# Output projection and the following norm as one stage, token tile by token tile

## What is computed

```
def rms_norm(x, g):
    return x * rsqrt(mean(x * x, axis=-1) + 1e-6) * g

for layer in (0, 1):
    x = x + gate_m * (mix(rms_norm(x, norm_mix) * (1 + sc_m) + sh_m) @ w_out)
    h = rms_norm(x, norm_ffn) * (1 + sc_f) + sh_f      # router and experts read h
    x = x + gate_f * experts(h)
x = rms_norm(x, final_norm)
x = x + hawk_heads(rms_norm(x, hawk_norm)) @ hawk_w_out
x = x + nsa_heads(rms_norm(x, nsa_norm)) @ nsa_w_out
return rms_norm(x, final_norm_2)
```

## Time and profile before

| | |
|---|---|
| median of 3 runs | 2257.58 us (2252.99 to 2258.18) |
| the profiled execution | 2263.83 us, of which the profile's span is 2261.9 |
| mean granted TensorE clock | 0.92 of full speed |
| TensorE busy | 1937.0 us, 86% of the span |
| VectorE busy | 675.9 us, 30% |
| ScalarE busy | 352.4 us, 16% |
| DMA | 592.37 MB, 262 GB/s on the mean |

### The profile page before, as it was taken

How to read it: one execution, slowest core, us unless ns; L and a number is a source line. 1 busy time by engine, 2 the same in 40 slices (tenths; PEclk the granted TensorE clock), 3 DMA queues, 4 the chain that set the end, 5 groups by cost and what they waited for, 6 DMA issues and landing times.

```text
span 2261.9 us, 28119 instructions
## 1 busy us (share of the span) xinstructions
PE 1937.0 (86%) x11730; PEld 1249.6 (55%) x11730; DVE 675.9 (30%) x1544; ACT 352.4 (16%) x696; POOL 7.8 (0%) x12
## 2 busy tenths in 40 slices
PE   6997777799999997698599999999379998889887
PEld 4654664465455453454366555555268884558753
DVE  1766442222221221451222212221422041411192
ACT  1112121111101010221111010111111221211160
POOL 0000000000000000000000000000000000000000
PEclk8997688899999999798699999999789999999889
DMA  9998031499999999432189999999574333156100
GB/s 356 379 290 309 37 114 75 202 428 430 428 430 428 428 429 412 175 112 110 40 376 428 430 428 429 429 429 428 214 259 158 129 136 140 25 129 211 56 1 28
DMA packets 161987, 592.37 MB, mean 262 GB/s; under 512 B 47596, under 2 KB 55408, under 8 KB 137216
## 3 DMA queue, kind: packets, MB, share of 16 engines
q1 hardware_dynamic: 127280, 561.64, 62.5%
q10 hardware_dynamic: 33488, 25.59, 3.5%
q0 software_dynamic: 1152, 4.19, 0.5%
HBM read 573.50 MB, written 17.89 MB: 261 GB/s over the span
## 4 chain that ended last, share of the span: by engine, by line
PE 56%; DMA 30%; DVE 7%; ACT 2%; issue 2%; SPq 1%; DVEq 1%; ACTq 0%; POOL 0%; PEldq 0%; POOLq 0%
DMA ring<-in_exp_w_dram 28%; PE bank L703 14%; PE bank L1810 9%; PE bank L794 6%; PE bank L692 5%; PE bank L1830 3%; PE bank L2019 2%; PE bank L1789 2%; PE bank L2009 1%; PE bank L399 1%; PE bank L406 1%; DMA ring<-in_ada_w_dram 1%; PE bank L712 1%; DMA taken_rows<-expert_out,route_rows 1%; PE bank L1819 1%
## 5 line engine op out<-in xcount | busy, mean ns | idle before, releaser
L1810 PE MATMUL bank<-ring,own_tokens 128*64 128x256 f32 x4096 | 468.1, 383 | 57.3 <-DMA ring<-in_exp_w_dram 54.2
L1810 PEld LDWEIGHTS bank<-ring,own_tokens 128*64 128x64 f32 x4096 | 303.2, 137 | 238.7 <-DMA ring<-in_exp_w_dram 99.7
L703 PE MATMUL bank<-hT,ring 128*128 128x256 f32 x1408 | 308.3, 381 | 5.1 <-ACTq L161 5.1
L703 PEld LDWEIGHTS bank<-hT,ring 128*128 128x128 f32 x1408 | 269.1, 191 | 42.7 <-issue 5.7
L1830 PE MATMUL bank<-ring,own_hiddenT 128*64 128x512 f32 x1024 | 233.9, 597 | 3.8 <-issue 0.3
L1920 DVE TENSOR_TENSOR own_hidden<-bank,own_silu 128x256 f32<-128x256 f32 x64 | 27.1, 424 | 481.8 <-ACT own_silu L1868 481.8
L1830 PEld LDWEIGHTS bank<-ring,own_hiddenT 128*64 128x64 f32 x1024 | 75.8, 136 | 120.4 <-issue 120.4
L1789 PE MATMUL bank<-xn_kept,member 128*64 128x512 f32 x528 | 129.5, 607 | 12.7 <-issue 12.7
L692 PE MATMUL bank<-ring,hT 128*128 128x512 f32 (+2 forms) x288 | 117.7, 570 | 0.0
L1868 ACT ACTIVATE own_silu<-bank 128x256 f32<-128x256 f32 x64 | 24.5, 383 | 555.8 <-PE bank L1810 555.8
L1819 PEld LDWEIGHTS bank<-kc,own_hidden 128*64 128x64 f32 x1024 | 72.2, 211 | 32.4 <-DVE own_hidden L1920 18.0
(11 more groups left out here) (559 smaller groups left out, 1869.0 us busy)
## 6 DMA issues: line engine op xcount, KB each, us to landing
ring<-in_exp_w_dram SPq DMA_DIRECT2D x192, 2048.0 KB, 21.9
ring<-in_ada_w_dram SPq DMA_DIRECT2D x24, 2048.0 KB, 16.5
ring<-in_hawk_w_in_dram SPq DMA_DIRECT2D x15, 2048.0 KB, 8.0
expert_out<-own_out ACTq DMA_DIRECT2D x128, 128.0 KB, 8.3
ring<-in_even_w_in_dram SPq DMA_DIRECT2D x7, 2048.0 KB, 19.0
ring<-in_gla_w_in_dram SPq DMA_DIRECT2D x6, 2048.0 KB, 20.6
ring<-in_nsa_w_in_dram SPq DMA_DIRECT2D x5, 2048.0 KB, 8.7
ring<-in_even_w_out_dram SPq DMA_DIRECT2D x2, 2048.0 KB, 19.7
```

What stands on the lines that cost most here:

```text
L703: last = nc.tensor.matmul(pair[m // 2][0:rows, (m % 2) * T:(m % 2 + 1) * T], w[:, k, m * P:m * P + rows], src[:, k, :], start=(k == 0), st ...
L1810: last = nc.tensor.matmul(bank[2 + q][halves[half], part * FE // 2:(part + 1) * FE // 2], own[:, q, k % 4, k // 4, :], w[:, k, cols], star ...
```

## The change

`out_stage` takes a fifth argument that says which norm follows, and does this norm in the same stage. TensorE's order is tile 0 half 0, tile 0 half 1, tile 1 half 0, then `turn(0)` (the 8 blocks of tile 0), then tile 1 half 1 and `turn(1)`. As both halves of a tile need different chunks, a chunk is given back only when tile 1 has used it. VectorE adds each half of a tile as it is finished and ScalarE squares it (512 columns, with their sum); the mean, the root and the reciprocal are made for each tile. The scaling of a tile is cut by columns between VectorE and ScalarE (512 and 512; 640 and 384 where the columns are strided). The turned blocks lie in banks 4 to 7, and each is carried out as 128 by 128 instead of 128 by 256. At the end of the kernel `turn` and `keep` fall away: VectorE scales a tile in two halves with the gain row, which is loaded at the start of the stage, and SP stores each tile with a DMA of 0.5 MB when it is ready, and waits for both at the end. Five stages go (three `norm_stage`, one `final_norm_stage`, `store_stage`), with their meetings of the engines. The places for a kernel that ends early (`last_stage`) go too; they aren't used.

```diff
@@ -769,7 +769,8 @@
-        def out_stage(c0, parts, src, gate):
+        def out_stage(c0, parts, src, gate, after):
...
                 gated = sb(st, "gated", [P, 512])
+                stat = sb(st, "out_stat", [P, TT, 4])
...
                     @block.sync
                     def _(sp):
                         fill_ring(sp, c0 + n - 1)
+                        if final:
+                            for t in range(TT):
+                                sp.wait_ge(normed.sem, normed.at(2 * t + 2))
+                                sp.dma_start(out[0, t * P:(t + 1) * P, :], x[:, t, :]).then_inc(stored.up(16), 16)
+                            sp.wait_ge(stored.sem, stored.n)
                     @block.tensor
                     def _(pe):
-                        for half in range(2):
+                        def out_part(t, half):
                             for i, (k0, nk) in enumerate(parts):
                                 c = c0 + half * len(parts) + i
-                                arrived(pe, c)
-                                w = slot(c)
-                                for t in range(TT):
-                                    for k in range(nk):
-                                        last = nc.tensor.matmul(bank[2 * half + t][:, :], src[:, k0 + k, t * P:(t + 1) * P],
-                                                                w[:, k, :], start=(k0 + k == 0), stop=(k0 + k == last_k))
-                                last.then_inc(chunk_used.up(), 1)
+                                if t == 0:
+                                    arrived(pe, c)
+                                for k in range(nk):
+                                    last = nc.tensor.matmul(bank[2 * half + t][:, :], src[:, k0 + k, t * P:(t + 1) * P],
+                                                            slot(c)[:, k, :], start=(k0 + k == 0), stop=(k0 + k == last_k))
+                                if t == TT - 1:
+                                    last.then_inc(chunk_used.up(), 1)
+                            if t < TT - 1:
+                                last.then_inc(part_ready.up(), 1)
+                        def turn(t):
+                            pe.wait_ge(normed.sem, normed.at(2 * t + 2))
+                            for k in range(KD):
+                                last = nc.tensor.transpose(turned_tile(t, k), xn[:, t, k * P:(k + 1) * P], ident)
+                                if k % 2:
+                                    last.then_inc(turned.up(), 1)
+                        out_part(0, 0)
+                        out_part(0, 1)
+                        out_part(1, 0)
+                        if not final:
+                            turn(0)
+                        out_part(1, 1)
+                        if not final:
+                            turn(1)
                     @block.vector
                     def _(dve):
-                        for half in range(2):
-                            dve.wait_ge(chunk_used.sem, used0 + (half + 1) * len(parts))
-                            for t in range(TT):
-                                part = bank[2 * half + t][:, :]
-                                if gate is not None:
-                                    nc.vector.tensor_tensor(gated[:, :], part, gate[:, half * 512:(half + 1) * 512], ALU.mult).then_inc(vector_steps.up(), 1)
-                                    dve.wait_ge(vector_steps.sem, vector_steps.n)
-                                    part = gated[:, :]
-                                xs = x[:, t, half * 512:(half + 1) * 512]
-                                nc.vector.tensor_tensor(xs, xs, part, ALU.add).then_inc(vector_steps.up(), 1)
+                        def add(t, half):
+                            if t < TT - 1:
+                                dve.wait_ge(part_ready.sem, part_ready.at(half + 1))
+                            else:
+                                dve.wait_ge(chunk_used.sem, used0 + (half + 1) * len(parts))
+                            part = bank[2 * half + t][:, :]
...
+                            nc.vector.tensor_tensor(xs, xs, part, ALU.add).then_inc(x_added.up(), 1)
+                            dve.wait_ge(x_added.sem, x_added.n)
+                        def scale(t):
+                            dve.wait_ge(squared.sem, squared.at(2 * t + 2))
+                            nc.vector.tensor_tensor(stat[:, t, 2:3], stat[:, t, 0:1], stat[:, t, 1:2], ALU.add).then_inc(summed.up(), 1)
+                            dve.wait_ge(root.sem, root.at(t + 1))
+                            nc.vector.reciprocal(stat[:, t, 2:3], stat[:, t, 3:4]).then_inc(inverse.up(), 1)
+                            dve.wait_ge(inverse.sem, inverse.n)
+                            if final:
+                                dve.wait_ge(row_in.sem, row_in.at(16))
+                                for half in range(2):
+                                    cols = slice(half * 512, (half + 1) * 512)
+                                    nc.vector.scalar_tensor_tensor(x[:, t, cols], x[:, t, cols], stat[:, t, 2:3], row[:, cols], ALU.mult, ALU.mult)\
+                                        .then_inc(normed.up(), 1)
+                            else:
+                                to, of = columns(t, 0, cut)
+                                nc.vector.tensor_scalar(to, of, stat[:, t, 2:3], None, ALU.mult).then_inc(normed.up(), 1)
...
+                        def keep(t):
+                            for k in (0, 1, 4, 5):
+                                dve.wait_ge(turned.sem, turned.at(4 * t + k // 2 + 1))
+                                to = dst[:, k, t * P:(t + 1) * P]
+                                if shift is None:
+                                    nc.vector.tensor_scalar(to, turned_tile(t, k), gain[:, k:k + 1], None, ALU.mult)
...
+                        add(0, 0)
+                        add(0, 1)
+                        scale(0)
+                        add(1, 0)
+                        if not final:
+                            keep(0)
+                        add(1, 1)
+                        scale(1)
+                        if not final:
+                            keep(1)
+                    @block.scalar
+                    def _(act):
+                        def square(t, half):
+                            act.wait_ge(x_added.sem, x_added.at(2 * t + half + 1))
+                            nc.scalar.activation(xn[:, t, half * 512:(half + 1) * 512], x[:, t, half * 512:(half + 1) * 512], ACT.Square,
+                                                 accum_out=stat[:, t, half:half + 1]).then_inc(squared.up(), 1)
+                        def scale(t):
+                            act.wait_ge(summed.sem, summed.at(t + 1))
+                            nc.scalar.activation(stat[:, t, 3:4], stat[:, t, 2:3], ACT.Sqrt, scale=1.0 / D, bias=EPS).then_inc(root.up(), 1)
+                            if not final:
+                                act.wait_ge(inverse.sem, inverse.at(t + 1))
+                                to, of = columns(t, cut, D)
+                                nc.scalar.activation(to, of, ACT.Identity, scale=stat[:, t, 2:3]).then_inc(normed.up(), 1)
+                        def keep(t):
+                            for k in (2, 3, 6, 7):
+                                act.wait_ge(turned.sem, turned.at(4 * t + k // 2 + 1))
+                                to = dst[:, k, t * P:(t + 1) * P]
...
+                        if final:
+                            act.dma_start(row[:, :], A[after["row"]].partition_broadcast(P)).then_inc(row_in.up(16), 16)
+                        square(0, 0)
+                        square(0, 1)
+                        scale(0)
+                        square(1, 0)
+                        if not final:
+                            keep(0)
+                        square(1, 1)
+                        scale(1)
+                        if not final:
+                            keep(1)
@@ -2603,7 +2737,7 @@
-                out_stage(first["hawk_out"], [(0, 8), (8, 6)], yT, None)
+                out_stage(first["hawk_out"], [(0, 8), (8, 6)], yT, None, {"gain": col("nsa_norm_2"), "shift": None, "dst": hT, "xn": None})
...
-                norm_stage(x, col("nsa_norm_2"), None, hT)
...
-                out_stage(first["nsa_out"], [(0, 8), (8, 2)], yT, None)
+                out_stage(first["nsa_out"], [(0, 8), (8, 2)], yT, None, {"row": "final_norm_2"})
...
-        def store_stage():
-            stored, start = signal("output_stored"), met.n
-            with Stage(whole, met) as block:
-                @block.sync
-                def _(sp):
-                    sp.wait_ge(met.sem, start)
-                    sp.dma_start(out[0].rearrange("(t p) d -> p t d", p=P), x[:, :, :]).then_inc(stored.up(16), 16)
-                    sp.wait_ge(stored.sem, stored.n)
...
-                out_stage(first[("even_out", "gla_out")[layer]], [(0, KD)], hT, gates[layer][:, 0, :])
...
```

(14 more changed lines are left out.)

35 lines of the change are left out of this document (30 added, 5 removed).

## The result

The changed kernel took 2242.14 us (median of 4 runs, 2238.4 to 2244.79), against 2257.88 for the kernel before, with a fourth execution of that one: the medians lie 15.7 us apart. The ratio is 0.9937 with a 95% interval of 0.992 to 0.9954, by which it is 14.2 us less (10.4 to 18.1). On another chip (first experiment) the ratio was 0.9922 (0.9909 to 0.9935), 17.6 us of 2259.61 (14.7 to 20.6), with medians 20.3 apart. The forecast was 19.8 us less, 2237.8: outside the first interval, inside the second.

What follows compares the result with a forecast made beforehand. PE carries 56% of the chain and DMA 30%; the change can win only in the last 11%, at four joints. Their 19.8 us off the 2257.58 median gave 2237.8 us, range 2228 to 2248.

Steps and rivals of the forecast that it cites:

- The path through the joints: Joints 0 and 1, last projection matmul to each layer's router: 7.95 us against 12.8, 4.8 us less at each.
- Joint 2: The serial chain between a projection and the nsa projections: 6.7 us against 10.8, 4.1 us less.
- The table load: At joint 2, the 1.28 us load leaves the path because tile 0's root takes it 20 us earlier.
- The late return of the ring's slots: Before the nsa projections: first slot back 17 us later, the others 0 to 12 us later, costing nothing.
- Joint 3: From VectorE's first add there to the end of the span: 6.65 us against 12.75, 6.1 us less.
- The sum over the joints: All four joints together: 4.8 + 4.8 + 4.1 + 6.1 = 19.8 us less.
- the one between the joints: Behind joints 0 and 1: a joint 5 us shorter moves the expert stream and all behind it by 5 us.
- the clock as a rival of both signs: Router to refill: layer 0 slower (2242.9) or layer 1 faster (2232.7); joint 2 could win 1.6 less; chance 0.27.
- the sign of its being wrong: An expert stage's first refill doesn't move with the joint, or TensorE waits at turn(0).
- No overlap: Tile 0's chain isn't ready when TensorE comes to turn(0); with 3 us at three joints, 2246; chance 0.04.
- swallowed: Transfer-bound expert stages swallow the gains of joints 0 and 1, leaving 10.2 us, 2247.4; chance 0.06.
- slower: One whole expert or more per layer at half clock, losing about 12 us each; two each, 2285.8; chance 0.02.

Runs made afterwards that it cites:

- first experiment: The changed kernel run again unaltered on another chip, the same run as e1; ratio 0.9922 to the kernel before.
- e1: The changed kernel again, nothing altered, on the same chip as the next runs; ratio 0.9922 to the kernel before, 17.6 us less.
- e2: The changed kernel with joints 0 and 1 put back as before the change; ratio 0.995 to the kernel before, 11.3 us less.
- e3: The changed kernel with joints 2 and 3 put back as before the change; ratio 0.9966 to the kernel before, 7.7 us less.
- e11: The changed kernel with tile 0's blocks turned behind the last projection matmul and the output stored in four DMAs; ratio 0.9916, 2235.71 us.
- the control: The changed kernel run again unaltered, the same run as e1; ratio 0.9922 to the kernel before.
- e9: The changed kernel with 8 more blocks, read by nobody, turned behind turn(1) at joints 0 and 1; a single execution took 2238.5 us.
- e7: The changed kernel with tile 0's blocks turned behind the last projection matmul and carried out behind tile 1's scaling; ratio 0.9916 to the kernel before.
- e12: The kernel before the change with unread products at joints 0 and 1, in the router and before the first expert; ratio 0.9981, 4.3 us less.

## Why the prediction was right or wrong

- *The path through the joints*: right, each a little small or large. Joints 0 and 1: 4.8 foretold, 5.2 and 5.3 in the profile. (7.1 where joint 1 has its faster form, but the 1.8 more are the clock at the start of the projection, no gain of the change.) Its terms: turn(0) 0.9, was 0.87; square 0.75, 0.73; scaling 1.05, 0.94; turn(1) 1.84 at half clock, 1.67 and 1.52, as the clock fell only during it (8 blocks wholly at half clock took 1.97 in e1's joint 1).
- *Joint 2*: 4.1 foretold, 4.9. The step that was off is turn(1) at half clock: it ran at full clock, 1.09 us instead of 1.84. The table load left the path, as said, and nothing like the 1.38 us of drain that the Trainium skill adds ("ScalarE: Activation LUTs", "What ACT_TABLE_LOAD costs") was won: turn(1) accounts for what joint 2 gained beyond the sum, and in the after trace the root stands at 1972.31, 0.01 behind the end of the load. The late return of the ring's slots cost nothing visible; no DMA wait stands in the nsa projections. The prediction's "at joint 2 the first 3 us of projection could run at half clock (1.6 less)" came true in this profile: 57.09 against 55.52.
- *Joint 3*: 6.1 foretold, 5.8. The store's 2.7 was 2.6. What was missing is a wait: VectorE took up the sum 1.22 us after its add instead of 0.86 at the other joints, 0.36 us later. In e2 it was 0.86, in all the other new ends 1.22; I have no cause for it. It would have made e2's end shorter, but its two stores took 2.9 us, and joint 3 there is 41.85. The Trainium skill, "DMA: Bandwidth & Descriptors", section "Anatomy of one DMA — SWDGE (gpsimd) path", would have a 0.5 MB store at an estimated 3.2 us; the trace has 2.6 and 2.0 for 0.25 MB. The page's fit is for transfers from gpsimd and these go out on SP's queue; its fixed part of 2.0 us is too large here.
- *The sum over the joints* was therefore 21.1 against 19.8. The *step that failed is the one between the joints*: "a joint that is 5 us shorter moves the stream and all behind it by 5 us", with the clock as a rival of both signs. That the experts don't swallow a shift is borne out by e3, 7.7 us faster with joints 0 and 1 alone. But the router isn't the same behind a shorter joint: it takes 2.1 us more in both layers. The start of layer 0's experts took 1.8 more as well, which e11, with 0.2, shows not to be bound to the joint. So in layer 0 the first refill moved by 1.2 us, not by 5; the prediction named a refill that doesn't move with the joint as the sign of its being wrong, and this comes near to it. I had priced the clock as luck, when a part of it follows from the change itself: I moved 8 of 16 blocks away and costed only their time, not what they did for the clock of the work behind them. The row at 390 to 391 showed the router at full clock in its first half, and nothing asked why. Of the rival's two layers, layer 0 went to the slower form by 4.0 us (foretold 5.1); layer 1's refill moved both ways. (Layer 1's 41.3 us in the prediction end with the first expert's products; its refill lay at 41.53.)
- *No overlap* and *swallowed* were wrong, as put; *slower* too: the second expert's products took 7.10 or 7.11 us, full clock, in both layers of every profile.
- *The total*, 14.2 and 17.6 us by the ratios, is 21.1 less about 4.0 in layer 0 and 1.6 (2.6 in the control) in the nsa projections, with layer 1's refill at between 1.8 later and 2.8 earlier. The measured 2242.1 lies 4.3 us above the forecast and 0.8 below the rival in which layer 0 takes its slower form (2242.9). That rival's mechanism is the nearer one, but that its number is so near is luck: the joints gave 1.3 us more than the sum, layer 0 lost 1.1 less than foretold, and losses in layer 1 and nsa, which it didn't count, made up for it. What the runs don't settle is what puts the clock at full or at half where joints 1 and 2, the nsa projections and the first experts begin.

## What to carry to other kernels

Where two stages meet on one serial chain and the engines around it are idle during the first stage, doing the chain by tiles takes its first part off the path; the sum from row durations was good to 0.5 us at three of the four joints and 0.8 at the other. Of work that is moved, cost also what it did to the TensorE clock for the work behind it: here 8 small blocks moved some 12 us ahead of the others made the router 2.1 us slower. And when a kernel scatters by 5 us and more from run to run, read the effect in distances between two instructions inside the profile, not in its span.

## What was not expected of the hardware

- The same 36-column router matmuls took 1.98 us for 16 at full clock and 3.63 at half, and at half clock they stayed from 377.5 to 385.3 with TensorE busy in 7.78 of 7.80 us. With 16 turned blocks in one row ahead of them they began at full clock (before, e2, e9); with 8, or with 8 and 8 some 3 us apart (e7), they did not. The same row of 16 ahead of the projection of joint 0 left that one at half clock in all fourteen profiles.
- Three sizes of the same store, SBUF to DRAM: 1 MB 4.0, 0.5 MB 2.6 (2.9 in e2), 0.25 MB 2.0 us from issue to landing.
- 16 blocks of 128 by 128 took 1.97 us at full clock (e12) and 3.67 at half, 8 took 1.04 to 1.09 and 1.97; the length of such a row tells the clock without any other view.
